# RWKV rounds of a hybrid block: compact right-hand sides, two products joined, the spreading done by VectorE

## The reference, cut to what matters

```python
def step(s, inp):                      # s: (heads, 64, 64), one step a token
    r_t, w_t, k_t, v_t, kk_t, a_t = inp
    sa = einsum('bhij,bhj->bhi', s, -kk_t)
    s = s * w_t[:, :, None, :] + sa[..., None] * (kk_t * a_t)[:, :, None, :] + v_t[..., None] * k_t[:, :, None, :]
    return s, einsum('bhij,bhj->bhi', s, r_t)
```

## Time and profile before

| what | us |
|---|---|
| median of 3 runs (lowest, highest) | 2579.45 (2575.8, 2582.72) |
| the profiled execution: its time, its span | 2581.92, 2580.1 |
| busy PE / DVE / ACT / POOL | 2522.1 / 1800.1 / 1347.0 / 789.2 |

### The profile page before, as it was taken

How to read it: one execution, slowest core, us unless ns; L and a number is a source line. 1 busy time by engine, 2 the same in 40 slices (tenths; PEclk the granted TensorE clock), 3 DMA queues, 4 the chain that set the end, 5 groups by cost and what they waited for, 6 DMA issues and landing times.

```text
span 2580.1 us, 47661 instructions
## 1 busy us (share of the span) xinstructions
PE 2522.1 (98%) x14114; PEld 2186.8 (85%) x14114; DVE 1800.1 (70%) x3076; ACT 1347.0 (52%) x2534; POOL 789.2 (31%) x604
## 2 busy tenths in 40 slices
PE   8999999999999999999999999999999999999998
PEld 7899998998788878887888888888888888888876
DVE  5567976454766656699986888888766666666656
ACT  5446544333555455444446666666655555555545
POOL 0001004433000000398988888888700000000000
PEclk9999999999999999999999999999999999999999
DMA  6665651000566656665555655555555555555564
GB/s 213 186 191 156 177 179 50 18 17 18 162 196 194 215 172 175 172 183 170 182 177 178 176 163 163 163 163 163 158 195 191 193 194 194 191 193 194 193 223 163
DMA packets 302042, 429.22 MB, mean 166 GB/s; under 512 B 26901, under 2 KB 234247, under 8 KB 300679
## 3 DMA queue, kind: packets, MB, share of 16 engines
q1 hardware_dynamic: 301959, 428.12, 53.4%
HBM read 423.82 MB, written 4.19 MB: 166 GB/s over the span
## 4 chain that ended last, share of the span: by engine, by line
PE 65%; issue 23%; POOL 7%; DVE 3%; DMA 1%; ACT 1%; SPq 0%; POOLq 0%; DVEq 0%; ACTq 0%
PE PS L429 14%; PE PS L837 9%; PE PS L838 9%; PE PS L839 9%; PE PS L431 7%; POOL w_lo L1298 7%; PE PS L421 2%; PE PS L423 2%; PE PS L422 2%; PE PS L801 2%; PE PS L650 1%; PE PS L659 1%; PE PS L611 1%; DMA raw<-in_peer_v 1%; DVE w_lo L1312 0%
## 5 line engine op out<-in xcount | busy, mean ns | idle before, releaser
L429 PE MATMUL PS<-act_both,w_hi 128*128 128x512 f32 x2720 | 965.4, 399 | 14.1 <-POOL w_lo L1298 11.9
L1312 DVE TENSOR_TENSOR w_lo<-raw,w_hi 128x512 fp32r<-128x512 f32 x1064 | 720.9, 703 | 238.7 <-ACT w_hi L865 235.5
L1298 POOL TENSOR_TENSOR w_lo<-raw,w_hi 128x512 fp32r<-128x512 f32 x512 | 668.4, 1321 | 575.1 <-ACT w_hi L1139 556.9
L865 ACT ACTIVATE w_hi<-raw 128x512 fp32r<-128x512 f32 x1064 | 635.9, 624 | 363.8 <-PE PS L477 145.0
L431 PE MATMUL PS<-act_both,w_lo 128*128 128x256 f32 x2550 | 714.4, 280 | 0.0
L429 PEld LDWEIGHTS PS<-act_both,w_hi 128*128 128x128 f32 x2720 | 508.1, 188 | 129.8 <-issue 11.8
L431 PEld LDWEIGHTS PS<-act_both,w_lo 128*128 128x128 f32 x2550 | 482.5, 189 | 2.5
L1139 ACT ACTIVATE w_hi<-raw 128x512 fp32r<-128x512 f32 x512 | 317.1, 630 | 237.4 <-PE PS L431 129.5
L837 PE MATMUL PS<-w_hi,act_both 128*128 128x512 f32 x1024 | 399.3, 390 | 5.5 <-DVE w_lo L1312 5.5
L839 PE MATMUL PS<-w_hi,act_both 128*128 128x512 f32 x1024 | 398.8, 389 | 0.0
L838 PE MATMUL PS<-w_lo,act_both 128*128 128x512 f32 x1024 | 398.8, 389 | 0.0
(11 more groups left out here) (267 smaller groups left out, 2704.5 us busy)
## 6 DMA issues: line engine op xcount, KB each, us to landing
raw<-in_peer_u SPq DMA_DIRECT2D x1024, 128.0 KB, 2.7
raw<-in_peer_v SPq DMA_DIRECT2D x256, 512.0 KB, 4.3
raw<-in_w_in SPq DMA_DIRECT2D x180, 512.0 KB, 3.7
raw<-in_w_out SPq DMA_DIRECT2D x32, 512.0 KB, 4.5
raw<-in_peer_w_q SPq DMA_DIRECT2D x128, 128.0 KB, 3.2
raw<-in_w_ret_branch SPq DMA_DIRECT2D x16, 512.0 KB, 3.8
raw<-in_w_rwkv_branch SPq DMA_DIRECT2D x16, 512.0 KB, 4.6
big<-in_x SPq DMA_DIRECT2D x2, 1024.0 KB, 6.2
```

The costliest lines, as they stand in the source:

```text
L429: last = pe.matmul(PS[:, bank, :], wh, act_both[:, kc, :, :].rearrange("p w n -> p (w n)"), start=start, stop=stop)
L865: act.activation(w_hi[:, slot % 2, hh * 512:(hh + 1) * 512], raw[:, slot, hh * 512:(hh + 1) * 512], ACT.Copy).then_inc(S["unit_hi"], 1)
L1298: pool.tensor_tensor(w_lo[:, k % 2, cols].rearrange("p (c s i) -> p c s i", c=4, s=4), u_part(k, 4 * hh, 4), w_hi[:, k % 2, cols].bitcast( ...
L1312: dve.tensor_tensor(w_lo[:, slot % 2, cols], raw[:, slot, cols], w_hi[:, slot % 2, cols].bitcast(f32), ALU.subtract).then_inc(S["unit_spli ...
```

## The change

The blocks that are zero anyway are no longer kept in the right-hand sides: AMc holds 64 columns for alpha (the sum of the two halves) and 64 for MV (the block of each head, by two ACT copies, negated), so that the product with Xt has 128 columns for each chunk. DVE spreads its result to the block-diagonal AS by multiplying with a mask (`bdmask`), two operations a group. FC holds bn and B1[.., 1, :] side by side in 64 columns each, made by DVE in level 0; one product AS0 x FC stands for L680 and L683. It signals `f` by itself, the remaining two products signal it again. Lm and B2 are made from it by four operations of 64 partitions. The outputs go to bank 3g, the state products to bank 3g + 1, B1's source is bank 3g + 2. The waits are changed to fit. The order within the other steps is as before.

```diff
-        AM = [two(d["AM"]) for d in place]
+        AMc = [d["AM"][:, 0:512].rearrange("p (n w c) -> p n w c", n=4, w=2) for d in place]
+        FC = [d["AM"][:, 512:1024].rearrange("p (n w c) -> p n w c", n=4, w=2) for d in place]
-        alpha_bd = [AM[g][:, :, 1, :] for g in range(2)]
+        alpha_bd = [one(d["AM"][:, 512:1024]) for d in place]
...
@@ TensorE, start of a round @@
+                    wait_past(pe, S[f"ye{g}"], i * 2)
+                    first_products(g, beta_bd, 0).then_inc(S[f"s1{g}"], 1)
                     wait_past(pe, S[f"st{g}"], i * 2)
-                    first_products(g, beta_bd, 0).then_inc(S[f"s1{g}"], 1)
-                    wait_past(pe, S[f"ye{g}"], i * 2)
                     first_products(g, kappa_bd, 1).then_inc(S[f"s1{g}"], 1)
...
@@ TensorE, after the levels @@
-                    pe.wait_ge(S[f"mvc{g}"], i + 1)
+                    pe.wait_ge(S[f"mvc{g}"], i * 2 + 2)
                     for n in range(4):
-                        last = pe.matmul(PS[:, 3 * g + 2 * (n // 2), (n % 2) * 256:(n % 2 + 1) * 256], Xt[g][:, n, :],
-                                         AM[g][:, n, :, :], start=True, stop=True)
+                        last = pe.matmul(piece(g, 0, n), Xt[g][:, n, :], AMc[g][:, n, :, :], start=True, stop=True)
                     last.then_inc(S[f"as{g}"], 1)
                 for g in range(2):
+                    pe.wait_ge(S[f"asc{g}"], i * 2 + 1)
+                    pe.wait_ge(S[f"fc{g}"], i + 1)
+                    for n in range(4):
+                        last = pe.matmul(piece(g, 1, n), AS[g][:, n, 0, :], FC[g][:, n, :, :], start=True, stop=True)
+                    last.then_inc(S[f"f{g}"], 1)
                     pe.wait_ge(S[f"asc{g}"], i * 2 + 2)
                     for n in range(4):
-                        pe.matmul(piece(g, 1, n), AS[g][:, n, 0, :], bn_[g][:, n, :], start=True, stop=True)
-                        pe.matmul(piece(g, 0, n), kn_[g][:, n, :], Vn[g][:, n, :], start=True, stop=False)
-                        pe.matmul(piece(g, 0, n), bn_[g][:, n, :], AS[g][:, n, 1, :], start=False, stop=True)
-                        last = pe.matmul(piece(g, 2, n), AS[g][:, n, 0, :], B1[g][:, n, 1, :], start=True, stop=True)
+                        pe.matmul(piece(g, 2, n), kn_[g][:, n, :], Vn[g][:, n, :], start=True, stop=False)
+                        last = pe.matmul(piece(g, 2, n), bn_[g][:, n, :], AS[g][:, n, 1, :], start=False, stop=True)
                     last.then_inc(S[f"f{g}"], 1)
...
@@ TensorE, outputs @@
-                    out = piece(g, 1, n)
+                    out = piece(g, 0, n)
...
-                            pe.wait_ge(S[f"fe{g}"], i * 4 + 4)
+                            pe.wait_ge(S[f"fe{g}"], i * 5 + 5)
...
-                            pe.matmul(piece(g, 0, n), Lm[g][:, n, :], state, start=True, stop=True).then_inc(S[f"ch{g}"], 1)
+                            pe.matmul(piece(g, 1, n), Lm[g][:, n, :], state, start=True, stop=True).then_inc(S[f"ch{g}"], 1)
...
@@ ScalarE @@
-                    act.activation(AM[g][:, :, 1, :], four(g, 1), ACT.Copy).then_inc(S[f"mvc{g}"], 1)
-                for g in range(2):
-                    act.wait_ge(S[f"as{g}"], i + 1)
-                    for q in range(2):
-                        act.activation(AS[g][:, 2 * q:2 * q + 2, :, :],
-                                       PS[:, 3 * g + 2 * q, :].rearrange("p (n w c) -> p n w c", n=2, w=2), ACT.Copy,
-                                       scale=-1.0).then_inc(S[f"asc{g}"], 1)
+                    for h in range(2):
+                        rows = slice(64 * h, 64 * h + 64)
+                        act.activation(AMc[g][rows, :, 1, :], one(PS[rows, 3 * g + 1, :])[:, :, 64 * h:64 * h + 64],
+                                       ACT.Copy, scale=-1.0).then_inc(S[f"mvc{g}"], 1)
...
@@ GpSimd @@
-                    wait_past(pool, S[f"as{g}"], i)
+                    wait_past(pool, S[f"f{g}"], i * 2)
...
@@ VectorE @@
-                    dve.tensor_copy(AM[g][:, :, 0, :], four(g, 0)).then_inc(S[f"va{g}"], 1)
+                    dve.tensor_reduce(AMc[g][:, :, 0, :], PS[:, 3 * g, :].rearrange("p (n h c) -> p n c h", n=4, h=2), AX.X,
+                                      ALU.add).then_inc(S[f"va{g}"], 1)
...
+                    if lv == 0:
+                        for g in range(2):
+                            dve.tensor_tensor(FC[g][:, :, 1, :], B1[g][:, :, 1, 0:64], B1[g][:, :, 1, 64:128], ALU.add)
+                            dve.wait_ge(S[f"bk{g}"], i * 2 + 1)
+                            dve.tensor_tensor(FC[g][:, :, 0, :], bn_[g][:, :, 0:64], bn_[g][:, :, 64:128], ALU.add).then_inc(S[f"fc{g}"], 1)
...
                 for g in range(2):
-                    dve.wait_ge(S[f"f{g}"], i + 1)
-                    dve.tensor_tensor(Lm[g], four(g, 1), eye4, ALU.add).then_inc(S[f"fe{g}"], 1)
+                    dve.wait_ge(S[f"as{g}"], i + 1)
+                    both = PS[:, 3 * g, :].rearrange("p (n w c) -> p n w c", n=4, w=2)
+                    for w in range(2):
+                        dve.tensor_tensor(AS[g][:, :, w, :].rearrange("p n (h c) -> p n h c", h=2), bc(both[:, :, w, :], 2, 2),
+                                          bc(bdmask.rearrange("p (h c) -> p h c", h=2), 4),
+                                          ALU.mult).then_inc(S[f"asc{g}"], 1)
+                for g in range(2):
+                    dve.wait_ge(S[f"f{g}"], i * 2 + 1)
+                    for h in range(2):
+                        rows, cols = slice(64 * h, 64 * h + 64), slice(64 * h, 64 * h + 64)
+                        dve.tensor_tensor(Lm[g][rows, :, cols], eye4[rows, :, cols], one(PS[rows, 3 * g + 1, :])[:, :, 0:64],
+                                          ALU.subtract).then_inc(S[f"fe{g}"], 1)
+                        dve.tensor_tensor(B2[g][rows, :, 0, cols], big[rows, i * 2 + (90 + g), :].rearrange("p (n t) -> p n t", n=4),
+                                          one(PS[rows, 3 * g + 1, :])[:, :, 64:128],
+                                          ALU.subtract).then_inc(S[f"fe{g}"], 1)
+                    dve.wait_ge(S[f"f{g}"], i * 2 + 2)
                     pe4 = pend[:, i * 8 + 4 * g:i * 8 + 4 * g + 4].unsqueeze(2).broadcast_to([P, 4, P])
-                    dve.tensor_tensor(B1[g][:, :, 0, :], four(g, 0), pe4, ALU.mult).then_inc(S[f"fe{g}"], 1)
+                    dve.tensor_tensor(B1[g][:, :, 0, :], four(g, 2), pe4, ALU.mult).then_inc(S[f"fe{g}"], 1)
-                    for h in range(2):
-                        rows = slice(64 * h, 64 * h + 64)
-                        dve.tensor_tensor(B2[g][rows, :, 0, 64 * h:64 * h + 64], one(PS[rows, 3 * g + 2, :])[:, :, 64 * h:64 * h + 64],
-                                          big[rows, i * 2 + (90 + g), :].rearrange("p (n t) -> p n t", n=4),
-                                          ALU.add).then_inc(S[f"fe{g}"], 1)
```

More of the change, by code:

```diff
@@ L1079, in _ @@
                         act.activation(big[rows, i * 2 + (114 + g), :].rearrange("p (n t) -> p n t", n=4),
-                                       PS[rows, 3 * g + 1, :].rearrange("p (n w t) -> p n w t", n=4, w=2)[:, :, h, :],
+                                       PS[rows, 3 * g, :].rearrange("p (n w t) -> p n w t", n=4, w=2)[:, :, h, :],
                                        ACT.Copy).then_inc(S[f"ye{g}"], 1)
@@ L1610, in pairs @@
                         if n == 1:
-                            dve.wait_ge(S[f"fe{g}"], i * 4 + 4)
-                        dve.scalar_tensor_tensor(St[g][:, n - 1, :], PS[:, 3 * g, n * P:(n + 1) * P],
+                            dve.wait_ge(S[f"fe{g}"], i * 5 + 5)
+                        dve.scalar_tensor_tensor(St[g][:, n - 1, :], PS[:, 3 * g + 1, n * P:(n + 1) * P],
                                                  pend[:, i * 8 + 4 * g + n:i * 8 + 4 * g + n + 1], B1[g][:, n, 0, :], ALU.mult,
```

## The result

The change makes the kernel faster: median 2566.07 us over 5 runs (2560.87 to 2568.36) against 2576.13 for before (2575.8 to 2582.72), ratio 0.995 with a 95% interval of 0.9939 to 0.996 (the two medians alone would give 0.9961). Forecast were 2564.9 us and 14.6 us less. The medians differ by 10.1 us, the means of the same runs by 12.7 and the profiled executions by 14.7 (span 2565.4 against 2580.1); with runs of one kernel spread over 7 us, the traces tell the parts more sharply than the medians do.

What follows compares the result with a forecast made beforehand. PE, busy 98% of the span, was taken to bound the kernel; 4 x 3.4 + 3 x 0.49 = 15.1 us, less 0.5, gave 14.6 us saved and 2564.9 us from a 2579.45 median, range 2559 to 2573.

Steps and rivals of the forecast that it cites:

- Narrow product: Xt x AM in each round on 128 columns instead of 256: 3.58 us become 1.79, 1.79 saved.
- narrow products take as long: Rival: weight load sets the pace, so the first product saves nothing; 7.4 us gain left, 2572 us; chance 3%.
- Join: Products with bn and B1 become one with FC: 8 fewer block products of 32, 1.79 us saved a round.
- ACT's two copies: ACT evacuates MV by two 64x256 copies, not one 128x512, before Xt x AM: costs 0.09 us, bounds 0 to 0.5.
- the spreads: Four DVE operations spread the first product's result, replacing ACT's four: FC product of g0 waits, costing 0.04 us.
- State operands: Lm, B2, B1 after F: DVE starts earlier, so PE's 0.49 us wait before g1's outputs goes in three rounds.
- FC additions: Four 128x256 DVE additions in level 0: hidden, 0.16 us to spare, 0.5 if started every 0.35; bounds 0 or 0.9 a round.
- 7. and 8.: AM by summing two halves instead of a copy, and waits moved to ACT's evacuation and POOL's preparation: both cost nothing.
- rival three: POOL's preparation, now beside DVE's state operands, holds them up; PE loses 3.9 us in rounds 0 to 2, 2576 us; 4%.
- the 0.5 kept back: Reserve for small unseen delays, taken off the 15.1 us total gain to leave 14.6 us.

Runs made afterwards that it cites:

- halves: Changed kernel, but ACT and DVE evacuate MV and the result side by side, replacing two ACT copies and four masked DVE operations: median 2565.83 us, ratio 0.9948.
- compact operands: Changed kernel with v and the result's MV part moved as 64 columns, result written by ACT and DVE: median 2564.63 us, ratio 0.9946, period 52.42.
- narrow_split: Changed kernel without the join; products needing only the alpha half go first and signal by themselves, state products follow: one run, round period 54.48 us.
- join_only: Changed kernel with the first product 256 columns wide again and evacuated by ACT, join kept: median 2570.26 us, ratio 0.9966, period 54.04.
- narrow_only: Changed kernel with the join undone: one signal, no FC additions, both spreads awaited before F: median 2574.75 us, ratio 0.9985, period 55.89.
- fc_twice: Changed kernel with four more FC additions on DVE in level 0, into unread spare memory: one run, round period 53.29 us.
- fc_early: Changed kernel with the four FC additions moved ahead of level 0's Wn: one run, round period 52.73 us.

## Why the prediction was right

The mechanism was right: PE's time in the rounds fell by the products saved and by the wait before the outputs of g1. By the terms:

1. *Narrow product.* 3.58 to 1.79 forecast. Seen are 3.53 before and 1.91 after (500.00 to 501.91), with the wait for the first spread and the restart of item 3 in it; 1.78 us for 16 instructions of 128 columns with no wait (MV in halves). Proportional to the columns, as taken from the earlier trace rows. By the two figures of the Trainium skill (TensorE: Matmul & The Clock Gate, Back-to-back issue gap) it would have been an estimated 0.3 us, and this kernel's f32 products don't agree. The prediction sets these figures against the join too, but the join drops whole instructions and doesn't hang on how their time depends on the columns. The compact operands show a floor just below: from 128 to 64 columns hardly anything is gained (109 against 112 ns). Whether the weight load sets it or another cost of each instruction, no run separates. My rival "narrow products take as long" was false for 256 to 128 and would have been true one step further.
2. *Join.* 1.79 forecast; narrow_split against the changed kernel 1.78.
3. and 4. *ACT's two copies and the spreads.* From MV's start to the first output 12.51 before and 9.39 after, 3.12 less; forecast 3.40. The terms off are these two: PE started Xt x AMc 2.02 us after MV, against 1.83 before, so 0.19 and not 0.09; and from there to the first output it took 7.37, not 7.19. What was missing in the second is PE's restart: after a wait the next product follows later than the usual 0.22 us. The same place in the kernel before, behind the wait, and in the changed kernel, without one (behind 517.09 and 509.21):

```profile
517.42 0.39 PE L691 MATMUL PS<-big 128*128 128x128 f32 x2
...
509.43 0.39 PE L694 MATMUL PS<-big 128*128 128x128 f32 x2
```

That is 0.33 against 0.22. In the changed kernel the four products of L681 behind their wait take 1.00 us (501.91 to L685 at 502.91) instead of 0.895, and L675's second group is 0.08 late by DVE's start (T' + 1.17, forecast 1.09). I had left this 0.1 us for each new wait out. The other 0.10, the late start of Xt x AMc, is seen but not explained: ACT's second copy ends at 499.85 and PE starts at 500.00, 0.15 later and not 0.05. With halves, which takes this first wait away, 0.30 came back: the forecast delay of 0.09, these 0.10, the 0.08 and some hundredths.
5. *State operands.* The wait before the outputs of g1 is gone: 3.73 - 3.12 = 0.61 us in three rounds, forecast 0.49; the difference is again the restart of 0.1 us, which goes with the wait. The last round, where no such wait was, saved 3.12. That it goes through the early signal is shown by narrow_split (gone, with the early signal and without the join), join_only (gone) and narrow_only (grown to 0.5 by the matmul row, 1.0 by its weight load, from 0.3 and 0.75).
6. *FC additions.* Hidden with 0.16 to 0.5 to spare by forecast; DVE stood 0.66 us behind them; the 0.34 between starts is at the low end of my bounds. fc_twice shows the cover and where it ends, fc_early that their place costs nothing.
7. and 8. No row shows a cost. POOL's preparation lay at 505.06 to 510.25, beside DVE's 64x256 operations at 0.41 to 0.42 us and L1621 at 0.69: rival three is refuted in that trace.

The sum: 15.07 by the terms, 14.6 with the 0.5 kept back, 14.25 in the rounds. The 0.28 too much in items 1 to 4 is 1.1 us in four rounds, the 0.1 too little in item 5 0.3 in three. So the reserve was near what was missing, but I had no mechanism for it, and that it fits is luck. So is part of the nearness of 2564.9 to the median: the forecast starts from a median of before of 2579.45, which with five runs is 2576.13.

One reading in the prediction is wrong: 6.9 us is the spread of single runs of before, not of their medians, so its bound for what the measurement can tell is wider than these runs ask for; the interval here, 0.9939 to 0.996, tells a difference of 0.5% from none.

Open is why the medians of before differ by 4 us between comparisons (2576.13 to 2580.26) with rounds that repeat to 0.1; the ratios, 0.995 and 0.9957, agree within their intervals.

## What to carry to other kernels

Count columns down only to the floor: here f32 products with 128 weight columns cost by their moving columns from 256 to 128 and not below, so two half-empty products are better joined to 128 than narrowed to 64. When evacuation gets an extra step (a spread, a mask), let the product that needs only its first part go first and signal by itself; without that order the narrow product's gain shrank from 1.9 to 0.5 us a round (narrow_split, narrow_only). The early signal alone, in the kernel before, was not run; 0.6 us a round is what came with it in join_only beyond the eight products. And add about 0.1 us for each wait that PE really meets, on top of the wait.

## What the runs showed of the hardware

The hold between DVE and POOL goes both ways: a DVE operation with two inputs in SBUF waited for POOL (1.33 and 1.60 us against 0.41 and 0.68), and a POOL operation that started 0.03 us after such a one was long itself (1.78 against 1.28 us); DVE operations with one input in PSUM kept their 0.41 and 0.69 us beside POOL. The Trainium skill (SBUF — State Buffer, Who interferes with whom) says that a VectorE instruction with two SBUF inputs and a GpSimd instruction that reads SBUF hold each other up, the later one waiting, and that one with at most one SBUF input does not. These traces agree on which operations meet. On who waits they don't decide at so small a distance: 1.8 us later in fc_twice POOL's instruction starts first by its row (482.26, L1312 at 482.29) and is still the long one (1.83 against 0.68 us).

A f32 instruction with 64 moving columns took 109 ns, with 128 112 ns, with 256 about 221.
